# Differential attention in a four-layer fp32 stack: rotation side by side, one row maximum per head, four heads transposed by VectorE through DRAM

## The chip, the cores and the metric

The kernel runs on one core of a Trainium2 chip. The metric is the device time of one execution in microseconds. Three runs of the kernel before took 889.67, 889.81 and 889.84 us.

## The reference

The program is a stack of layers on 256 tokens of width 1024, all in fp32: gated linear attention, a feed-forward block, a gated projection, **differential attention**, a second feed-forward block and gated projection, a short convolution and a causal attention with ALiBi. The change lies in the differential attention, which is:

```python
q, k, v = split_cols(h @ w_in, [D_MODEL, D_MODEL, D_MODEL])
q = rms_norm(q.reshape(bsz, seq, nh, 2, dh), g_q)
k = rms_norm(k.reshape(bsz, seq, nh, 2, dh), g_k)
q = rope(...); k = rope(...)
lam = exp(sum(lam_q1 * lam_k1)) - exp(sum(lam_q2 * lam_k2)) + lambda_init
s = einsum('bhtqd,bhtkd->bhtqk', q_blk, kt) * scale
pr = softmax(s, axis=-1)
a = pr[:, :, 0] - lam * pr[:, :, 1]
o = einsum('bhqk,bhkd->bhqd', a, vt)
o = rms_norm(o, g_sub) * (1.0 - lambda_init)
return o.reshape(bsz, seq, D_MODEL) @ w_out
```

There are 8 heads (nh), each with two softmax maps of 256 x 256 (the index t, in the kernel m) over 64 columns, and values of 128 columns.

## The kernel before

**The weight stream.** Every matrix is cut into units of 256 rows by 512 columns (128 partitions x 1024 elements, 512 KB). For each unit SyncE loads `raw`, ScalarE rounds it to `whi` (L719, line function `split_to`), VectorE writes the rest `wlo = raw - whi` (L1130), and TensorE runs 12 matmuls of 512 columns (L1867, `product`): two row blocks and two column blocks of the activations, each as whi by hi, wlo by hi and whi by lo. ScalarE may not write a `whi` until TensorE is done with the unit 8 before it (RING = 8, semaphore `w_used`). A unit takes TensorE about 2.7 us, and there are 295.

**The order of the differential attention.** Its stage has 24 units of the input projection (six tiles of four: q, k, k, q, v, v halves) and 8 of the output projection. What else each engine has to do there is written out by hand in `DF_ORDER`: (u, step, argument) for each of TensorE (`pe`), ScalarE (`act`), VectorE (`dve`) and GpSimd (`pool`). TensorE does its steps ahead of unit u. ScalarE first writes `whi` up to unit u+6, VectorE `wlo` up to unit u+5, and then the step. Each engine runs its list strictly in that order, so a step that has to wait holds back all that stands behind it.

**The steps.** A tile of the projection (`tile`, L803 and L791) is squared and copied by ScalarE to `df_tok`. VectorE sums the squares (`sums`, L1524), GpSimd raises the sums to the power -0.5 (L644), and VectorE rotates the tile (`rope` and `more`: one row block of 128 tokens each, in `df_rope`, L1534 to L1554). For one row block this is two multiplications by the sine (256 elements, L1548), one by the cosine (512, L1552) and an addition (512, L1554), of which each kind waits for the one before it. k tiles are also scaled (`unit`, L1531). TensorE transposes the tiles (`qkT`, L2142), and ScalarE copies them from PSUM to `df_qkT` (L963).

Then, for each head: TensorE computes `scores` (L2156, eight matmuls into two banks, one per map); VectorE takes the maximum of each map (L1572, 512 elements from PSUM) and scales it (L1575); ScalarE runs four exponentials (L976, 256 elements each); VectorE combines the two maps (`soft`, L1582 to L1588); TensorE transposes the result (`aT`, L2167, four matmuls of 128 columns into bank 6); ScalarE copies it to `df_aT` (L984, `df_copy`), and TensorE multiplies by the values (`av`, L2182). Pairs of heads are then squared, copied and normalised (ScalarE's step `av`, `osums`, `norm`), transposed (`pair`, L1920) and split into hi and lo (ScalarE L730, VectorE L1146), and these are the left side of the output projection, whose first unit is u = 24.

**Banks.** Even heads use PSUM banks 4 and 5 for their scores, odd heads the pair of banks that the projection's other tiles leave free. Whoever writes a bank next waits for its reader (`claim`): the scores of head 2 for the exponentials of head 0, unit 24 for those of head 7, and so on.

**The other way to transpose.** The last attention of the stack already takes the probabilities of some of its heads (`MB_TRIPS`) another way: VectorE transposes blocks of 32 x 32 (L1740), GpSimd's queue writes the tile to DRAM (L673) and reads it back with the blocks in their new places (L681). `pair_blk` (L1171) does such a transpose of a 128 x 256 tile for the residual.

## Time and profile before

| | |
|---|---|
| median of three runs | 889.81 us (889.67 to 889.84) |
| profiled execution, span from first to last instruction | 888.3 us |
| median of the runs less that span | 1.5 us |
| busy: TensorE, VectorE, ScalarE, GpSimd | 99%, 76%, 57%, 8% |
| granted TensorE clock over the span | 1.000 |
| differential attention: first to last unit on TensorE | about 321 to 436 us |

A busy share is that of the time between an instruction's start and end in the trace. Instructions of one engine overlap a little: the next one's record starts before the last one's ends. So a cost is read from the start of one instruction to the start of the next. Times in the rows below are from the start of the span. "x4" in a timeline means that four instructions of one kind were merged into one row.

### The profile page before, as it was taken

What the parts mean: (1) busy time and instruction counts of PE and PEld (TensorE: products, weight loads), DVE (VectorE), ACT (ScalarE), POOL (GpSimd) and SP (SyncE); (2) the same over time, 40 slices, a digit from 0 to 9 for tenths busy, and PEclk for the clock granted to TensorE, in tenths of its full rate; (3) what the DMA queues carried; (4) which work ended last, traced back from release to release, by engine and by line L of the source; (5) the groups of instructions that cost most, each with busy time, mean ns of one, the idle gap of its engine ahead of it and who ended that gap; (6) DMA issues with size and microseconds to landing.
All of it is one profiled execution on the core that took longest, in us unless ns stands there. A gap on an engine that the chain in (4) does not pass through costs nothing.

```text
span 888.3 us, 12034 instructions
## 1 busy us (share of the span) xinstructions
PE 883.2 (99%) x4292; PEld 729.1 (82%) x4292; DVE 671.3 (76%) x1039; ACT 503.3 (57%) x822; POOL 75.4 (8%) x88
## 2 busy tenths in 40 slices
PE   9999999999999999999999999999999999999998
PEld 8988888888888878778888888888888888887777
DVE  6997688666746699997786666646879987789763
ACT  7656464444535576887564444444765444577581
POOL 1002000000000403111100000000010000115200
PEclk9999999999999999999999999999999999999999
DMA  9754578776666666433387667665787774857501
GB/s 341 263 179 176 203 260 297 251 267 246 241 213 237 213 227 246 144 103 112 131 300 265 250 235 255 244 233 178 254 296 261 239 245 144 300 175 238 186 26 48
DMA packets 85059, 193.72 MB, mean 218 GB/s; under 512 B 7236, under 2 KB 38340, under 8 KB 85000
## 3 DMA queue, kind: packets, MB, share of 16 engines
q1 hardware_dynamic: 83544, 189.15, 60.3%
q0 software_dynamic: 1024, 3.15, 1.0%
q8 instruction: 34, 0.56, 0.2%
q10 hardware_dynamic: 432, 0.66, 0.2%
q14 instruction: 25, 0.20, 0.1%
HBM read 174.84 MB, written 18.09 MB: 217 GB/s over the span
## 4 chain that ended last, share of the span: by engine, by line
PE 96%; DVE 1%; DMA 1%; ACT 0%; issue 0%; DVEq 0%; ACTq 0%
PE bank L1867 86%; PE bank L1905 3%; PE bank L2156 1%; PE bank L2182 1%; PE bank L2262 1%; PE bank L2292 1%; PE bank L1920 1%; DMA h<-x_dram 0%; DMA h_land<-residual_blocks 0%; PE bank L2167 0%; PE bank L2248 0%; PE bank L2067 0%; PE bank L2071 0%; PE bank L2142 0%; PE bank L2272 0%
## 5 line engine op out<-in xcount | busy, mean ns | idle before, releaser
L1130 DVE TENSOR_TENSOR wlo<-raw,whi 128x1024 fp32r<-128x1024 f32 x295 | 346.5, 1212 | 34.4 <-ACT whi L719 34.1
L719 ACT ACTIVATE whi<-raw 128x1024 fp32r<-128x1024 f32 x295 | 301.6, 1059 | 114.5 <-PE bank L1867 98.6
L1867 PE MATMUL bank<-whi,x_hi 128*128 128x512 f32 x560 | 152.4, 394 | 0.0
L1867 PE MATMUL bank<-wlo,x_hi 128*128 128x512 f32 x560 | 149.9, 389 | 0.0
L1867 PE MATMUL bank<-whi,x_lo 128*128 128x512 f32 x560 | 149.8, 389 | 0.0
L1867 PEld LDWEIGHTS bank<-wlo,x_hi 128*128 128x128 f32 x560 | 105.1, 188 | 22.2
L1867 PEld LDWEIGHTS bank<-whi,x_lo 128*128 128x128 f32 x560 | 105.1, 188 | 21.9
L1867 PEld LDWEIGHTS bank<-whi,x_hi 128*128 128x128 f32 x560 | 103.6, 188 | 22.5 <-issue 1.8
L1867 PE MATMUL bank<-whi,y_hi 128*128 128x512 f32 x396 | 107.6, 393 | 0.1
L1867 PE MATMUL bank<-whi,y_lo 128*128 128x512 f32 x396 | 106.1, 390 | 0.0
L1867 PE MATMUL bank<-wlo,y_hi 128*128 128x512 f32 x396 | 106.0, 389 | 0.0
L1867 PEld LDWEIGHTS bank<-whi,y_lo 128*128 128x128 f32 x396 | 74.3, 188 | 16.1 <-DVE y_lo L1146 0.5
L1867 PEld LDWEIGHTS bank<-wlo,y_hi 128*128 128x128 f32 x396 | 74.3, 188 | 15.7
L1867 PEld LDWEIGHTS bank<-whi,y_hi 128*128 128x128 f32 x396 | 73.1, 188 | 15.7 <-issue 0.8
L881 ACT ACTIVATE ffn_silu<-bank,rstd 128x256 f32<-128x256 f32 x44 | 18.4, 470 | 78.7 <-PE bank L1867 78.7
L1376 DVE SCALAR_TENSOR_TENSOR ffn_mid<-bank,rstd,ffn_silu 128x256 f32<-128x256 f32 x44 | 19.3, 479 | 54.9 <-ACT ffn_silu L881 54.7
L600 POOL TENSOR_TENSOR ms<-stats 128x2 f32<-128x2 f32 x8 | 4.9, 613 | 561.6 <-ACT junk L771 561.6
L1867 PE MATMUL bank<-whi,mid_hi 128*128 128x512 f32 x176 | 47.0, 389 | 0.0
L1867 PE MATMUL bank<-wlo,mid_hi 128*128 128x512 f32 x176 | 47.0, 389 | 0.0
L1867 PE MATMUL bank<-whi,mid_lo 128*128 128x512 f32 x176 | 47.0, 389 | 0.0
L1867 PEld LDWEIGHTS bank<-whi,mid_lo 128*128 128x128 f32 x176 | 33.0, 188 | 6.9
L1867 PEld LDWEIGHTS bank<-whi,mid_hi 128*128 128x128 f32 x176 | 33.0, 188 | 6.8
(260 smaller groups left out, 888.0 us busy)
## 6 DMA issues: line engine op xcount, KB each, us to landing
raw<-stream_dram SPq DMA_DIRECT2D x295, 512.0 KB, 4.6
ffn_blocks<-ffn_blk SPq DMA_DIRECT2D x22, 256.0 KB, 2.2
ffn_land<-ffn_blocks SPq DMA_DIRECT2D x22, 256.0 KB, 4.1
residual_blocks<-h_blk SPq DMA_DIRECT2D x20, 256.0 KB, 2.0
h_land<-residual_blocks SPq DMA_DIRECT2D x20, 256.0 KB, 2.8
cv_blocks<-cv_blk SPq DMA_DIRECT2D x7, 256.0 KB, 3.6
cv_land<-cv_blocks SPq DMA_DIRECT2D x7, 256.0 KB, 3.2
h_blocks<-h_blk SPq DMA_DIRECT2D x3, 512.0 KB, 2.9
```

The lines of the kernel that those rows point to most:

```text
L600: step(nc.gpsimd.tensor_tensor(ms[:, j, 0, :], stats[:, j, 0, :], stats[:, j, 1, :], ALU.add))
L719: A(whi[:, u % RING, :], raw[:, u % SLOTS, :], ACT.Copy).then_inc(sem("w_hi"), 1)
L881: A(sg[:, (t - tin) % 2, k, :], bank[2 * (t % 2) + k][:, 0:256], ACT.Silu, scale=rstd[:, j, k:k + 1]).then_inc(sem("ffn_silu"), 1)
L1130: V.tensor_tensor(wlo[:, u % SLOTS, :], raw[:, u % SLOTS, :], whi[:, u % RING, :].bitcast(F32), ALU.subtract).then_inc(sem("w_lo"), 1)
L1376: V.scalar_tensor_tensor(mid[:, (t - tin) % 2, :, k, :], bank[2 * (t % 2) + k][:, 256:512].rearrange("p (k n) -> p k n", k=2), rstd[:, j, ...
L1867: last = T.matmul(bank[pair + t][:, :], lhs[a][:, kt, t * P:(t + 1) * P], w[:, place(w, u), kk * NW:(kk + 1) * NW], start=part != 1 and k ...
L1905: last = T.matmul(bank[pair + hd // 2][:, hd % 2 * SEQ:(hd % 2 + 1) * SEQ], w[:, place(w, u), kk * NW + hd * P:kk * NW + (hd + 1) * P], lh ...
L1920: last = T.transpose(bank[b][:, k * SEQ + t * P:k * SEQ + (t + 1) * P], src[:, t, kt * P:(kt + 1) * P], ident)
L2156: last = T.matmul(bank[DF_S_BANKS[hd][m]][:, q * SEQ:(q + 1) * SEQ], dT[r, 0, hd, q * P:(q + 1) * P], dT[r, 1, hd, :], start=True, stop=True)
L2182: last = T.matmul(bank[b][:, q * SEQ + (hd % 2) * P:q * SEQ + (hd % 2 + 1) * P], daT[:, hd % 4, k * SEQ + q * P:k * SEQ + (q + 1) * P], dv ...
L2262: last = T.matmul(bank[MB_S_BANKS[i][m]][:, (0, P)[q]:(P, 3 * P)[q]], mT[r, 0, i, q * P:(q + 1) * P], mT[r, 1, i, 0:(q + 1) * P], start=Tr ...
L2292: last = T.matmul(bank[7][m * MB_HD:(m + 1) * MB_HD, c0 + k * P:c0 + SEQ], mv[:, k, hd * MB_HD:(hd + 1) * MB_HD], mpT[:, hd % 4, 2 * k * P ...
```

## The change

- **Trips.** The transposes of heads 0, 2, 3 and 4 on TensorE (16 of the 32) and their bank are dropped. VectorE transposes these heads' maps in blocks of 32 x 32 (`blk`, two instructions of 128 x 256 for each head), GpSimd's queue writes them to DRAM (`out`) and reads them back (`in`), 256 KB each way, and ScalarE copies them from the landing tile in SBUF to `df_aT` instead of from bank 6. The landing tile lies over a part of `x_lo`, and the tile that is written out over `p_hi` and `p_lo`.
- **Rotation.** `more` is gone: both row blocks of a tile are rotated in one step, the four sine multiplications first, then the two by the cosine, then the two additions. For tile 1 the step now stands behind `sums`, for tile 3 it stands whole ahead of head 1's `soft` and head 3's maximum.
- **Row maximum.** The eight banks become one PSUM tensor, and one reduction per head runs over both banks (1024 elements, four results), followed by one scaling. The exponentials of a head wait for both maps.
- **Order.** TensorE's `qkT` 5 moves next to `qkT` 4, and `aT` 1 from u = 18 to 19. ScalarE's copies of heads 0 to 4 move later: that of head 2 behind the exponentials of head 6, that of head 3 behind those of head 7, and that of head 4 behind `tile` 5 and `av` 3.
- The last attention's trips use the same semaphores and count on from the four new ones.

```diff
+DF_TRIPS = (0, 2, 3, 4)
+DF_TURNED = tuple(_h for _h in range(8) if _h not in DF_TRIPS)
...
 DF_ORDER = {
     "pe": (
         (1, "second", 0), (11, "qkT", 0), (11, "qkT", 1), (12, "qkT", 2), (13, "scores", 0), (13, "qkT", 3),
-        (13, "scores", 1), (16, "scores", 2), (16, "aT", 0), (18, "qkT", 4), (18, "scores", 3), (18, "aT", 1),
-        (19, "qkT", 5), (20, "qkT", 6), (20, "qkT", 7), (20, "scores", 4), (20, "aT", 2), (21, "scores", 5),
-        (21, "av", 0), (21, "aT", 3), (21, "av", 1), (21, "scores", 6), (22, "scores", 7), (22, "aT", 4),
+        (13, "scores", 1), (16, "scores", 2), (18, "qkT", 4), (18, "qkT", 5), (18, "scores", 3),
+        (19, "aT", 1), (20, "qkT", 6), (20, "qkT", 7), (20, "scores", 4), (21, "scores", 5),
+        (21, "av", 0), (21, "av", 1), (21, "scores", 6), (22, "scores", 7),
         (24, "pair", 0), (24, "av", 2), (24, "av", 3), (25, "aT", 5), (25, "av", 4), (25, "aT", 6), (25, "av", 5),
         (25, "aT", 7), (26, "pair", 1), (26, "av", 6), (26, "av", 7), (27, "pair", 2), (28, "pair", 3),),
     "act": (
         (5, "tile", 0), (8, "tile", 1), (11, "qkT", 0), (12, "qkT", 1), (12, "tile", 2), (12, "qkT", 2),
-        (13, "qkT", 3), (14, "scores", 0), (15, "scores", 1), (16, "tile", 3), (16, "aT", 0), (16, "scores", 2),
-        (18, "qkT", 4), (18, "aT", 1), (18, "scores", 3), (18, "qkT", 5), (19, "qkT", 6), (19, "qkT", 7),
-        (20, "tile", 4), (20, "scores", 4), (20, "aT", 2), (20, "scores", 5), (20, "aT", 3), (21, "av", 1),
-        (21, "scores", 6), (21, "aT", 4), (24, "scores", 7), (24, "pair", 0), (24, "tile", 5), (24, "av", 3),
-        (24, "aT", 5), (25, "aT", 6), (26, "av", 5), (26, "aT", 7), (26, "pair", 1), (27, "av", 7), (28, "pair", 2),
+        (13, "qkT", 3), (14, "scores", 0), (15, "scores", 1), (16, "tile", 3), (16, "scores", 2),
+        (18, "qkT", 4), (18, "qkT", 5), (18, "aT", 0), (18, "scores", 3), (19, "aT", 1), (19, "qkT", 6), (19, "qkT", 7),
+        (20, "tile", 4), (20, "scores", 4), (20, "scores", 5), (21, "av", 1),
+        (21, "scores", 6), (22, "aT", 2), (24, "scores", 7), (24, "aT", 3), (24, "pair", 0), (24, "tile", 5), (24, "av", 3),
+        (24, "aT", 4), (24, "aT", 5), (25, "aT", 6), (26, "av", 5), (26, "aT", 7), (26, "pair", 1), (27, "av", 7), (28, "pair", 2),
         (28, "pair", 3),),
     "dve": (
-        (5, "rope", 0), (6, "more", 0), (6, "sums", 0), (8, "rope", 1), (8, "sums", 1), (8, "more", 1),
-        (9, "unit", 1), (11, "sums", 2), (11, "rope", 2), (11, "more", 2), (11, "scores", 0), (12, "scores", 1),
-        (13, "soft", 0), (16, "unit", 2), (17, "scores", 2), (17, "soft", 1), (17, "rope", 3), (17, "scores", 3),
-        (17, "sums", 3), (17, "more", 3), (18, "soft", 2), (19, "scores", 4), (19, "soft", 3), (19, "scores", 5),
-        (19, "soft", 4), (21, "scores", 6), (22, "osums", 0), (22, "scores", 7), (22, "norm", 0), (22, "soft", 5),
+        (5, "rope", 0), (6, "sums", 0), (8, "sums", 1), (8, "rope", 1),
+        (9, "unit", 1), (11, "sums", 2), (11, "rope", 2), (11, "scores", 0), (12, "scores", 1),
+        (13, "soft", 0), (13, "blk", 0), (16, "unit", 2), (17, "scores", 2), (17, "rope", 3), (17, "soft", 1), (17, "scores", 3),
+        (17, "sums", 3), (18, "soft", 2), (18, "blk", 2), (19, "scores", 4), (19, "soft", 3), (19, "blk", 3), (19, "scores", 5),
+        (19, "soft", 4), (19, "blk", 4), (21, "scores", 6), (22, "osums", 0), (22, "scores", 7), (22, "norm", 0), (22, "soft", 5),
         (22, "soft", 6), (23, "pair", 0), (23, "osums", 1), (23, "soft", 7), (24, "norm", 1), (25, "osums", 2),
         (25, "pair", 1), (26, "norm", 2), (27, "osums", 3), (27, "norm", 3), (27, "pair", 2), (28, "pair", 3),),
     "pool": (
-        (4, "sums", 0), (8, "sums", 1), (12, "sums", 2), (16, "sums", 3), (21, "osums", 0), (24, "osums", 1),
+        (4, "sums", 0), (8, "sums", 1), (12, "sums", 2), (13, "out", 0), (14, "in", 0), (16, "sums", 3), (18, "out", 2), (19, "out", 3), (19, "in", 2),
+        (20, "in", 3), (20, "out", 4), (21, "osums", 0), (21, "in", 4), (24, "osums", 1),
         (26, "osums", 2), (28, "osums", 3),),
 }
+DF_COPIED = tuple(arg for _, step, arg in DF_ORDER["act"] if step == "aT")
...
-        bank = [ctx.enter_context(nc.psum_tensor(f"bank{b}", [P, NW], F32)) for b in range(8)]
+        psum = ctx.enter_context(nc.psum_tensor("bank", [P, 8, NW], F32))
+        bank = [psum[:, b, :] for b in range(8)]
...
+        sb("under_df_land", [P, 3 * D], scope=landing)
+        aland = sb("df_land", [P, 2, NW], scope=landing)
...
+        ablk = sb("df_blk", [P, 2, NW], scope=staging)
...
+            def df_out(hd):
+                n = DF_TRIPS.index(hd)
+                pool.wait_ge(sem("mb_blk"), n + 1)
+                nc.gpsimd.dma_start(a_dram[n], ablk[:, n % 2, :]).then_inc(sem(f"mb_out{n % 2}"), 16)
+            def df_in(hd):
+                n = DF_TRIPS.index(hd)
+                pool.wait_ge(sem(f"mb_out{n % 2}"), 16 * (n // 2 + 1))
+                if n >= 2:
+                    pool.wait_ge(sem("df_aT"), DF_COPIED.index(DF_TRIPS[n - 2]) + 1)
+                nc.gpsimd.dma_start(aland[:, n % 2, :].rearrange("p (i w) -> p i w", i=P // B),
+                                    a_dram[n].rearrange("q n -> (q n)").rearrange("(i p w) -> p i w", i=P // B, p=P))\
+                    .then_inc(sem(f"mb_land{n % 2}"), 16)
...
+            def turned_aside(hd):
+                if hd in DF_TRIPS:
+                    act.wait_ge(sem("mb_blk"), DF_TRIPS.index(hd) + 1)
+                else:
+                    act.wait_ge(sem("df_aT_filled"), DF_TURNED.index(hd) + 1)
             def df_exp(hd):
                 if DF_P_AFTER[hd] is not None:
-                    act.wait_ge(sem("df_aT_filled"), DF_P_AFTER[hd] + 1)
+                    turned_aside(DF_P_AFTER[hd])
                 elif hd == 6:
                     act.wait_ge(sem("df_rope"), TT * 4)
                 for m in range(2):
-                    act.wait_ge(sem("df_max"), 4 * hd + 2 * (m + 1))
+                    act.wait_ge(sem("df_max"), 2 * (hd + 1))
...
             def df_copy(hd):
-                act.wait_ge(sem("df_aT_filled"), hd + 1)
                 if hd >= 4:
                     act.wait_ge(sem("df_av"), hd - 3)
+                if hd in DF_TRIPS:
+                    n = DF_TRIPS.index(hd)
+                    act.wait_ge(sem(f"mb_land{n % 2}"), 16 * (n // 2 + 1))
+                    A(daT[:, hd % 4, :].rearrange("p (n i b) -> p n i b", n=4, b=B),
+                      aland[:, n % 2, :].rearrange("p (i n b) -> p n i b", n=4, b=B), ACT.Copy).then_inc(sem("df_aT"), 1)
+                    return
+                act.wait_ge(sem("df_aT_filled"), DF_TURNED.index(hd) + 1)
                 A(daT[:, hd % 4, :], bank[6][:, :], ACT.Copy).then_inc(sem("df_aT"), 1)
...
-            def df_rope(t, k):
+            def df_rope(t):
                 w = (0, 1, 1, 0)[t]
-                for k in (k,):
-                    xt = dtok[:, t % 2, k, :]
-                    x5 = xt.rearrange("p (a m u e) -> p a m u e", a=4, m=2, u=2)
+                for k in range(TT):
+                    x5 = dtok[:, t % 2, k, :].rearrange("p (a m u e) -> p a m u e", a=4, m=2, u=2)
                     m5 = dm2[:, k, :].rearrange("p (a m u e) -> p a m u e", a=4, m=2, u=2)
                     sn = rot[:, w, 1, k, :].rearrange("p (m u e) -> p m u e", m=2, u=2)
-                    cs = rot[:, w, 0, k, :].unsqueeze(1).to_broadcast([P, 4, P])
-                    x3 = xt.rearrange("p (a e) -> p a e", a=4)
                     dve.wait_ge(sem("df_in"), TT * t + k + 1)
                     if t:
                         dve.wait_ge(sem("df_rope"), TT * (t - 1) + k + 1)
@@ -1548,8 +1591,13 @@
                         V.tensor_tensor(m5[:, :, :, u, :], x5[:, :, :, 1 - u, :],
                                         sn[:, :, u, :].unsqueeze(1).to_broadcast([P, 4, 2, HD2]), ALU.mult)\
                             .then_inc(sem("df_swap"), 1)
+                for k in range(TT):
+                    x3 = dtok[:, t % 2, k, :].rearrange("p (a e) -> p a e", a=4)
                     dve.wait_ge(sem("df_swap"), 2 * (TT * t + k + 1))
-                    V.tensor_tensor(x3, x3, cs, ALU.mult).then_inc(sem("df_cos"), 1)
+                    V.tensor_tensor(x3, x3, rot[:, w, 0, k, :].unsqueeze(1).to_broadcast([P, 4, P]), ALU.mult)\
+                        .then_inc(sem("df_cos"), 1)
+                for k in range(TT):
+                    xt = dtok[:, t % 2, k, :]
                     dve.wait_ge(sem("df_cos"), TT * t + k + 1)
                     V.tensor_tensor(xt, xt, dm2[:, k, :], ALU.add).then_inc(sem("df_rope"), 1)
@@ -1564,16 +1612,18 @@
             def df_max(hd):
                 stt = dstat[:, hd, :]
-                factors = dqr[:, hd // 4, :].rearrange("p (q a m) -> p q a m", q=TT, a=4)
+                factors = dqr[:, hd // 4, :].rearrange("p (q a m) -> p a m q", q=TT, a=4)
                 if hd % 4 == 0:
                     dve.wait_ge(sem("df_rstd"), TT * (1, 4)[hd // 4])
-                for m in range(2):
-                    dve.wait_ge(sem("df_scores"), 2 * hd + m + 1)
-                    V.tensor_reduce(stt[:, 2 * m:2 * m + 2], bank[DF_S_BANKS[hd][m]][:, :].rearrange("p (q k) -> p q k", q=TT),
-                                    AXX, ALU.max).then_inc(sem("df_max"), 1)
-                    dve.wait_ge(sem("df_max"), 4 * hd + 2 * m + 1)
-                    V.scalar_tensor_tensor(stt[:, 4 + 2 * m:6 + 2 * m], stt[:, 2 * m:2 * m + 2], -1.0,
-                                           factors[:, :, hd % 4, m], ALU.mult, ALU.mult).then_inc(sem("df_max"), 1)
+                b = DF_S_BANKS[hd][0]
+                dve.wait_ge(sem("df_scores"), 2 * (hd + 1))
+                V.tensor_reduce(stt[:, 0:4].rearrange("p (m q) -> p m q", m=2),
+                                psum[:, b:b + 2, :].rearrange("p m (q k) -> p m q k", q=TT), AXX, ALU.max)\
+                    .then_inc(sem("df_max"), 1)
+                dve.wait_ge(sem("df_max"), 2 * hd + 1)
+                V.scalar_tensor_tensor(stt[:, 4:8].rearrange("p (m q) -> p m q", m=2),
+                                       stt[:, 0:4].rearrange("p (m q) -> p m q", m=2), -1.0,
+                                       factors[:, hd % 4, :, :], ALU.mult, ALU.mult).then_inc(sem("df_max"), 1)
...
+            def df_blocks(hd):
+                n = DF_TRIPS.index(hd)
+                dve.wait_ge(sem("df_a"), TT * (hd + 1))
+                if n >= 2:
+                    dve.wait_ge(sem(f"mb_out{n % 2}"), 16 * (n // 2))
+                for q in range(TT):
+                    last = V.transpose(ablk[:, n % 2, :].rearrange("p (f k q b) -> p q f k b", f=P // B, q=TT, b=B)[:, q],
+                                       DF_P[hd][:, 0, q, :].rearrange("p (k b f) -> p f k b", b=B, f=P // B))
+                last.then_inc(sem("mb_blk"), 1)
```

## Rows read from the trace of the kernel before

**Rows 1.** The page: the chain that ended last, shares of the span by engine.
```profile
PE 96%; DVE 1%; DMA 1%; ACT 0%; issue 0%; DVEq 0%; ACTq 0%
```

**Rows 2.** Timeline of TensorE: start us, us, engine, line, operation, count, idle before.
```profile
386.10 1.14 PE L2156 MATMUL bank<-df_qkT 64*128 64x256 f32 x8 [0.25 <-ACT df_qkT L963]
...
398.03 1.13 PE L2156 MATMUL bank<-df_qkT 64*128 64x256 f32 x8
399.10 0.66 PE L2167 MATMUL bank<-consts,df_p 128*128 128x128 f32 x4
399.51 1.17 PE L1867 MATMUL bank<-whi,y_hi 128*128 128x512 f32 x4
...
405.50 1.95 PE L2182 MATMUL bank<-df_v,df_aT 128*128 128x128 f32 x16
407.21 1.17 PE L1867 MATMUL bank<-whi,x_hi 128*128 128x512 f32 x4
```

**Rows 3.** Timeline of ScalarE, same columns as rows 2.
```profile
356.70 1.27 ACT L791 ACTIVATE df_tok<-bank,rstd 128x512 f32<-128x512 f32 x2
...
377.81 2.00 ACT L719 ACTIVATE whi<-raw 128x1024 fp32r<-128x1024 f32 x2
...
380.65 0.59 ACT L976 ACTIVATE df_o<-bank,df_stat,df_q_rstd 128x256 f32<-128x256 f32 x1
...
385.44 1.09 ACT L963 ACTIVATE df_qkT<-bank 128x512 f32<-128x512 f32 x2 [1.04 <-PE bank L2142]
...
397.79 0.56 ACT L976 ACTIVATE df_m<-bank,df_stat,df_q_rstd 128x256 f32<-128x256 f32 x1 [0.33 <-DVE df_stat L1575]
...
400.45 3.22 ACT L719 ACTIVATE whi<-raw 128x1024 fp32r<-128x1024 f32 x3
403.57 0.55 ACT L976 ACTIVATE df_p<-bank,df_stat,df_q_rstd 128x256 f32<-128x256 f32 x1
...
405.74 0.84 ACT L730 ACTIVATE x_hi<-bank,cols 128x256 fp32r<-128x256 f32 x2
```

**Rows 4.** Timeline of VectorE, same columns.
```profile
357.63 0.75 DVE L1548 TENSOR_TENSOR df_m<-df_tok,df_rot 128x256 f32<-128x256 f32 x2
358.41 0.69 DVE L1552 TENSOR_TENSOR df_tok<-df_tok,df_rot 128x512 f32<-128x512 f32 x1
359.13 0.69 DVE L1554 TENSOR_TENSOR df_tok<-df_tok,df_m 128x512 f32<-128x512 f32 x1
359.74 0.75 DVE L1548 TENSOR_TENSOR df_m<-df_tok,df_rot 128x256 f32<-128x256 f32 x2
...
361.86 0.68 DVE L1572 TENSOR_REDUCE df_stat<-bank 128x2 f32<-128x512 f32 x1
...
363.45 1.22 DVE L1130 TENSOR_TENSOR wlo<-raw,whi 128x1024 fp32r<-128x1024 f32 x1
...
381.28 1.30 DVE L1524 TENSOR_REDUCE df_ss<-df_sq 128x8 f32<-128x520 f32 x2
...
391.68 0.69 DVE L1572 TENSOR_REDUCE df_stat<-bank 128x2 f32<-128x512 f32 x1 [0.60 <-PE bank L2156]
...
398.41 1.22 DVE L1130 TENSOR_TENSOR wlo<-raw,whi 128x1024 fp32r<-128x1024 f32 x1
...
431.60 1.14 DVE L1171 STREAM_TRANSPOSE h_blk<-h 128x256 f32<-128x256 f32 x2
```

**Rows 5.** Stretch: us, busy PE, PEld, DVE, ACT, POOL (instructions), clock, DMA share, GB/s.
```profile
357.60:399.80 42.20, 41.95 (x234) 32.27 (x233) 40.41 (x83) 35.56 (x86) 6.41 (x4) 1.00 0.35 121
```

**Rows 6.** Groups by line with shapes kept apart: count, busy us, mean ns, idle before.
```profile
L741 ACT ACTIVATE y_hi<-h_land,cols 128x256 fp32r<-128x256 f32 x12 | 5.5, 503 | 9.0 <-DMA h_land<-residual_blocks 9.0
...
L1727 DVE TENSOR_REDUCE mb_stat<-mb_s 128x1 f32<-128x128 f32 x16 | 4.6, 286 | 0.6
```

**Rows 7.** DMA issues by line: KB each, median us from issue to landing.
```profile
mb_blocks<-p_tok POOLq DMA_DIRECT2D x8, 192.0 KB, 3.4
mb_pT<-mb_blocks POOLq DMA_DIRECT2D x8, 192.0 KB, 4.1
```

More of the change, by code:

```diff
@@ L651, in df_onorm @@
                     .then_inc(sem("df_orstd"), 1)
-            for _, what, arg in df_order("pool"):
-                if what == "sums":
+            def df_out(hd):
[10 more added lines that the diff above has]
+                    .then_inc(sem(f"mb_land{n % 2}"), 16)
+            for _, what, arg in df_order("pool"):
+                if what == "out":
+                    df_out(arg)
+                elif what == "in":
+                    df_in(arg)
+                elif what == "sums":
                     for k in range(TT):
@@ L1611, in _ @@
                     head_sums(arg, dsq65, dss, "df_sq", "df_ss", "df_rstd")
-                elif step in ("rope", "more"):
-                    df_rope(arg, step == "more")
+                elif step == "rope":
+                    df_rope(arg)
                 elif step == "unit" and arg in (1, 2):
@@ L1622, in _ @@
                     df_soft(arg)
+                elif step == "blk":
+                    df_blocks(arg)
                 elif step == "osums":
@@ L1734, in mb_blocks @@
             def mb_blocks(hd):
-                n = MB_TRIPS.index(hd)
+                n = len(DF_TRIPS) + MB_TRIPS.index(hd)
                 dve.wait_ge(sem("mb_exp"), TT * (hd + 1))
@@ L2280, in mb_av @@
                 if 2 * i in MB_TRIPS:
-                    pair = MB_TRIPS.index(2 * i) // 2
+                    pair = (len(DF_TRIPS) + MB_TRIPS.index(2 * i)) // 2
                     pe.wait_ge(sem(f"mb_land{pair % 2}"), 2 * 16 * (pair // 2 + 1))
```

21 lines of the change are left out of this document (13 added, 8 removed).

## The prediction

> **What bounds the kernel now.** I read the page's chain first: TensorE carries 96% of it [rows 1], so one microsecond taken off TensorE in the attention stage is one gained, and one for which TensorE must wait is one lost. Then I read TensorE's own timeline in the stage. It stands still once, ahead of head 4's scores, for ScalarE's copy of transpose 6: the copy starts at 385.44 and the scores at 386.10 [rows 2, 3]. Nothing else there waits. Last I read the engines that feed it. From the rotation of tile 2 at 357.63 to the last maximum before 398.41, VectorE has one pause, 0.60 us ahead of head 5's maximum, and is busy 40.41 of 42.20 us [rows 4, 5]. So VectorE paces the chain of small steps, although TensorE does not notice yet. The tight place is unit 24, the first of the output projection. Its weights start at 407.21 [rows 2]; it needs head 7's exponentials out of the banks, which end at 405.74, and the first pair's hi parts, which ScalarE writes from 405.74 on [rows 3]: 0.84 us, so until 406.6. The slack is 0.6 us.
>
> **The change, part by part.**
>
> *TensorE.* After a head's scores a transpose takes 399.10 to 399.51, 0.41 us [rows 2]. Four go: -1.66 us (a fourth one, between two products with the values, costs much the same). Moving transpose 5 next to 4 I put at nothing; it saves or costs one change of operation, 0.1 us.
>
> *Rotation.* An instruction that reads the one before it starts 0.03 us after that one's end (357.63 + 0.75 = 358.38, start 358.41; 358.41 + 0.69 = 359.10, start 359.13); one that does not starts 0.08 us ahead of the end (359.13 + 0.69 = 359.82, start 359.74) [rows 4]. Side by side, all four dependences of a tile are covered: -4 x 0.11 = -0.44 us for each tile. The Trainium skill ("VectorE: DVE Perf Modes", section "The DRAIN you can't avoid") says that the next instruction does not start until the pipe is empty, and that chaining without semaphores gains nothing; by that the rotation would save nothing. The trace does not bear it out here, since the addition's successor started ahead of its end; I keep -0.44.
>
> *Maximum.* A head's two now take 361.86 to 363.45, 1.59 us [rows 4]. A reduction takes 0.286 us for 128 elements [rows 6] and 0.68 for 512, 1.03 ns an element, so an estimated 1.21 for 1024; with the dependent scaling 1.21 + 0.03 + 0.08 = 1.32. That is -0.27 a head. Bounds: no saving in the reduction beyond one scaling and its edges (-0.2), or half of the fixed part again (-0.35). But the first exponential now waits for both maps.
>
> *Blocks.* Two transposes of 128 x 256 take 1.14 us [rows 4]; behind the softmax they are dependent: 1.14 - 0.08 + 0.11 = 1.17 a head, four times.
>
> *Copies.* From PSUM, 512 elements follow each other in 0.49 us (two in 1.09) [rows 3]. From a landing tile in SBUF only 256 are seen, 0.503 us [rows 6]. To the 1024 of a whi copy (two in 2.00, so 1.05 each, 0.95 apart) [rows 3] it rises by 0.71 ns an element: 0.69 us, 0.59 to the next. Bounds 0.49 and 0.95; I take 0.59, the row with the same broken pattern.
>
> *Trips.* 3.4 us out and 4.1 back for 192 KB [rows 7]; here 256 KB, so an estimated 3.4 to 4.5 and 4.1 to 5.5. GpSimd's list is in order: `in` 2 waits behind `out` 3, which goes when head 3's blocks are done, at 392.4 by the sum below; it lands by 398. Head 3's own waits for its `out`: 402.4 at the latest. ScalarE comes for the two at 403.0 and 407.7 (below). Head 4's has some 1.5 us to spare (rival 4). GpSimd's powers for tile 3 come 10 us after `in` 0 and lose nothing. I take nothing for trips. SyncE's queue is unchanged; the four last-attention trips that share semaphores wait for counts long reached.
>
> *Start of the count.* The sums of tile 1 now wait for GpSimd's powers of tile 0, which eats what rotations 0 and 1 save. Rotation 2 cannot start before ScalarE writes the tile, 356.70 to 357.97 [rows 3], so I start at 357.63 as before, -0.2 to +0.5.
>
> *VectorE up to head 6's maximum.* It ended at 398.41 [rows 4]. Rotations 2 and 3: -0.88. Seven maxima: -1.89. Blocks of heads 0, 2, 3, 4: +4.68. The pause of 0.60 [rows 4] goes. Together +1.31: 399.72. Splits for units 25 and 26 still stand ahead of it. The exponentials of head 6 follow about 0.18 later, at 399.9, against 397.79 [rows 3]. That is the step which pays: ScalarE has nothing else it may do, since its next whi stands behind them.
>
> *ScalarE from there to unit 24.* Four exponentials 2.17 (403.57 to 405.74) [rows 3]: 402.07. One whi 0.95: 403.02. Copy of head 2, 0.59: 403.61. Two whi 1.90: 405.51 (before, three took 3.12 because the last waited for unit 22; by now that is long done). Head 7's exponentials 2.17: 407.68. Copy of head 3, new in this place, 0.69: 408.37. TensorE can then do `av` 3, eight of the sixteen matmuls that took 405.50 to 407.21 [rows 2], 0.86 us, 0.05 after the copy: unit 24 at 409.28. The pair's hi parts come at 408.27 + 0.84 = 409.11 and do not decide.
>
> So unit 24 starts **2.07 us later** than 407.21, though TensorE had 1.66 us less to do. A second stall lies on the way: rotation 3 ahead of head 3's maximum, which ended at 381.28 [rows 4]. Its second half +2.12 (357.63 to 359.74 is one half [rows 4]), blocks of head 0 +1.17, rotations -0.88, four maxima -1.08: 382.61. Exponentials 382.8 instead of 380.65 [rows 3], +2.17, whi +0.95, copy of head 1 +0.49, copy of transpose 6 +0.66: head 4's scores at 387.1 instead of 386.10. With the transposes gone this alone would put unit 24 at 407.21 + 0.94 - 1.24 = 406.9. It is inside the 2.07, not beside it: the later of the two chains decides. Behind unit 24 the spacing stays, and TensorE has no slack in which to make it up.
>
> The sum: 889.81 + 2.07 = **891.9 us**. The durations are of one execution with a span of 888.3 us; the runs lie 1.5 us above it, and I add the difference to their median. For this forecast alone I put 890.9 to 893.0 (reductions +-0.08 for each of seven heads, copies between their bounds, start of the count).
>
> **The rivals.**
>
> 1. *TensorE alone decides.* VectorE and ScalarE keep up and neither wait appears: -1.66 us, 888.2. This is the gain side. For it: VectorE's list has grown by only 1.3 us in 42. Against: head 6's exponentials would have to start by 399.9 - 2.07 - 1.66 = 396.2, ahead of where they start today, with 4.68 us more to do. To come past 0.2% the wait at head 4's scores would have to shrink too. 0.16, of which 0.09 beyond 0.2%.
>
> 2. *Only the first stall.* Copies or blocks come cheaper, so that `av` 3 does not wait, but head 4's scores still do: 406.9 for unit 24, -0.3, 889.5. It needs head 6's exponentials by 397.5. Everything from here to the forecast is a mixture of the two. 0.22.
>
> 3. *Dependences cost the same wherever they stand.* In rows: the second cosine and the additions start 0.03 us after the end of the one ahead, not 0.08 before it; rotations 2 and 3 save nothing, +0.88 in front of head 6, 892.8. The rows above speak against it. The Trainium skill's page "VectorE: DVE Perf Modes" states it in the section "The DRAIN you can't avoid". 0.08.
>
> 4. *A trip lands late.* Head 4's `in` waits for ScalarE's copy of head 2 (done 403.7) and lands 4.1 to 5.5 later, 409.2 with GpSimd's issue to add. ScalarE wants it behind the pair (0.8), tile 5 (1.2, as 356.70 shows) and two passes over a bank (1.0) after 408.3 [rows 3]: 411.3. If it slips by 3 us, the copy of head 4 and `av` 4 behind it come some 1.5 later: 893.4. 0.06.
>
> The forecast itself has 0.48.
>
> **How the numbers follow.** A measurement of this kernel can tell about 0.2%, 1.78 us, from no change: slower means above 891.6, faster below 888.0. The forecast's 0.48 lies above 891.6 in some two thirds (0.31), 3 and 4 wholly (0.14), and of the mixture next to nothing: slower 0.45. Rival 1 gives faster 0.09. The rest, 0.46, is within 0.2%. The range leaves out the outer half of rival 1 and the slip beyond 893.2: 888.6 to 893.2.
>
> **What would show it.** Right: a wait of TensorE on `df_aT` ahead of `av` 3, of 2 us or more, and one of about 1 us more than before on `df_qkT`; head 6's exponentials at about 399.9 after an idle ScalarE that waits for `df_stat`; VectorE without a pause from 357 to 400; tiles in SBUF before ScalarE reaches their copies; one reduction at 1.2 us. Wrong: no wait at `av` 3; head 6's exponentials before 398; a DMA named as what ended ScalarE's wait; reductions of two banks that cost clearly other than 1.2 us, or a rotation that takes 4.2 us as before.

## The result and the profile after

The changed kernel took **893.22 us** in the median (891.34 to 893.83, 6 runs) against 889.83 us (889.65 to 890.24, 6 runs) of the kernel before beside it: ratio 1.0030, 95% interval [1.0020, 1.0039]. That is 3.4 us slower, at the upper edge of the range given (893.2). The runs fall in two bunches, 891.34 and 891.61 us at a mean granted clock of 1.000, and 893.1 to 893.5 at 0.998; the profiled one (893.83 us, span 892.0) belongs to neither, for a reason of its own below.

In the page's chain TensorE's share fell from 96% [rows 1] to 90%, and VectorE's rose from 1% to 7%:

```profile
PE 90%; DVE 7%; issue 1%; ACT 1%; DMA 1%; POOL 0%; ACTq 0%; DVEq 0%
```

The timeline of TensorE in the attention stage, changed kernel (start us, us, engine, line, operation, count, idle before and who ended it); the first row is unit 11's weights, the last unit 24's:

```profile
354.50 1.17 PE L1930 MATMUL bank<-whi,y_hi 128*128 128x512 f32 x4
...
383.68 0.63 PE L2230 MATMUL bank<-consts,df_p 128*128 128x128 f32 x4 [0.28 <-ACT df_qkT L996]
...
388.60 0.63 PE L2205 MATMUL bank<-consts,df_tok 128*128 128x128 f32 x4 [1.08 <-ACT df_aT L1030]
389.15 1.13 PE L2219 MATMUL bank<-df_qkT 64*128 64x256 f32 x8
...
407.29 1.06 PE L2245 MATMUL bank<-df_v,df_aT 128*128 128x128 f32 x8
410.34 1.16 PE L2245 MATMUL bank<-df_v,df_aT 128*128 128x128 f32 x8 [1.99 <-ACT df_aT L1026]
411.27 1.16 PE L1930 MATMUL bank<-whi,x_hi 128*128 128x512 f32 x4
```

Where before there was one pause of 0.25 us [rows 2] there are three: 0.28 us ahead of head 1's transposes, 1.08 us ahead of transpose 7 (its bank is held by head 1's transposed map until ScalarE has copied it), and 1.99 us ahead of head 3's product with the values, for the copy of head 3. From unit 11's weights to unit 24's it takes 411.27 - 354.50 = **56.77 us**. Before, unit 11's weights started at 352.48 and unit 24's at 407.21 [rows 2]: 54.73. I call this the stretch from here on; it is what a run changed in the stage, whatever came before. Unit 11 in the kernel before:

```profile
352.48 1.17 PE L1867 MATMUL bank<-whi,y_hi 128*128 128x512 f32 x4
```

What made the copy late is read backwards on ScalarE (same columns):

```profile
401.93 0.57 ACT L1016 ACTIVATE df_m<-bank,df_stat,df_q_rstd 128x256 f32<-128x256 f32 x1 [1.72 <-DVE df_stat L1624]
...
405.06 0.63 ACT L1026 ACTIVATE df_aT<-df_land 128x512 f32<-128x512 f32 x1
405.57 2.01 ACT L752 ACTIVATE whi<-raw 128x1024 fp32r<-128x1024 f32 x2
407.47 0.56 ACT L1016 ACTIVATE df_p<-bank,df_stat,df_q_rstd 128x256 f32<-128x256 f32 x1
...
409.63 0.65 ACT L1026 ACTIVATE df_aT<-df_land 128x512 f32<-128x512 f32 x1
```

Head 6's exponentials (401.93) waited 1.72 us for VectorE's maximum; everything down to the copy of head 3 at 409.63 then runs without a pause. On VectorE:

```profile
359.68 1.42 DVE L1591 TENSOR_TENSOR df_m<-df_tok,df_rot 128x256 f32<-128x256 f32 x4
361.01 1.28 DVE L1597 TENSOR_TENSOR df_tok<-df_tok,df_rot 128x512 f32<-128x512 f32 x2
362.22 1.28 DVE L1602 TENSOR_TENSOR df_tok<-df_tok,df_m 128x512 f32<-128x512 f32 x2
363.42 1.21 DVE L1620 TENSOR_REDUCE df_stat<-bank 128x4 f32<-128x1024 f32 x1
364.67 0.17 DVE L1624 SCALAR_TENSOR_TENSOR df_stat<-df_stat,df_q_rstd 128x4 f32<-128x4 f32 x1
364.75 1.22 DVE L1176 TENSOR_TENSOR wlo<-raw,whi 128x1024 fp32r<-128x1024 f32 x1
...
397.09 1.16 DVE L1648 STREAM_TRANSPOSE df_blk<-df_p 128x256 f32<-128x256 f32 x2
398.18 2.32 DVE L1176 TENSOR_TENSOR wlo<-raw,whi 128x1024 fp32r<-128x1024 f32 x2
400.41 1.22 DVE L1620 TENSOR_REDUCE df_stat<-bank 128x4 f32<-128x1024 f32 x1
```

The three kinds of step can be priced here against [rows 4]: a rotation takes 363.42 - 359.68 = 3.74 us, a head's maximum 364.75 - 363.42 = 1.33 us. Head 6's maximum starts at 400.41, behind head 4's blocks and two splits.

**The start of this execution.** Unit 11 came 2.02 us later than before (354.50 against 352.48), though nothing that TensorE runs before it was changed. It comes from the first microseconds. Changed kernel:

```profile
1.17 3.78 PE L2029 MATMUL bank<-gla_r 128*128 128x256 f32 x8 [1.17 <-DVE gla_r L1261]
5.82 1.09 PE L1983 MATMUL bank<-consts,h 128*128 128x128 f32 x4 [0.86 <-DMA h<-x_dram]
6.70 1.92 PE L2039 MATMUL bank<-gla_r 128*128 128x256 f32 x4
8.05 2.27 PE L1968 MATMUL bank<-x_hi,whi 128*128 128x256 f32 x8
```

Kernel before:

```profile
5.28 1.01 PE L1920 MATMUL bank<-consts,h 128*128 128x128 f32 x4 [0.32 <-DMA h<-x_dram]
6.13 1.03 PE L1976 MATMUL bank<-gla_r 128*128 128x256 f32 x4
6.94 1.22 PE L1905 MATMUL bank<-x_hi,whi 128*128 128x256 f32 x8
```

The first tile landed 0.54 us later, the same four products then took 1.92 us instead of 1.03, and the eight behind them 2.27 instead of 1.22. A second profile of the same changed kernel (E12) starts like the kernel before, so I take 2.02 us off the times of this profile when I compare them with the prediction's.

### The profile page after: what moved, and what is told of

It reads as the page before. It is cut to its first block, busy times and chain, and to the rows that moved or that the text cites. A ratio compares the mean times of both kernels' runs of the same rounds, so it can differ in the third digit from the quotient of the medians.

```text
span 892.0 us, 12004 instructions
## 1 busy us (share of the span) xinstructions
PE 883.8 (99%) x4276; PEld 729.0 (82%) x4276; DVE 672.8 (75%) x1031; ACT 504.1 (57%) x822; POOL 81.8 (9%) x96
## 4 chain that ended last, share of the span: by engine, by line
PE 90%; DVE 7%; issue 1%; ACT 1%; DMA 1%; POOL 0%; ACTq 0%; DVEq 0%
PE bank L1930 81%; PE bank L1968 3%; DVE wlo L1176 2%; DVE df_stat L1620 1%; PE bank L2325 1%; PE bank L2355 1%; DVE df_m L1591 1%; PE bank L1983 1%; DMA h<-x_dram 1%; DVE df_tok L1597 1%; PE bank L2245 1%; POOL df_q_rstd L657 0%; DVE df_blk L1648 0%; DVE df_tok L1602 0%; PE bank L2311 0%
```

## The experiments

All times are medians, and each ratio is against runs of the kernel before on the same chip. Four chips were used: one for E1 to E4, one for E5 to E8, one for E9 and E10, one for E11 and E12; the medians of the kernel before on them are 890.10, 889.97, 889.74 and 889.79 us. "Stretch" is read from each run's own trace.

**E1. More warm-up products.** Do the late start of the profile and the two bunches of runs have one cause?

```
-WARM, KEEP = 4, 2
+WARM, KEEP = 6, 2
```

> The changed kernel with six warm-up products instead of four ahead of the first load; nothing else. In the trace of the changed kernel TensorE waited 0.86 us for the first tile instead of 0.32, and the products after it took twice as long: the attention stage (weights of unit 11) began at 354.50 instead of 352.48 us. Theory: the gap before the first tile is what costs, and two thirds of the excess is slow products. Filled, unit 11 begins within 0.7 us of 352.48 and all runs lie within 0.6 us of 891.6. Rival: the late landing of the first tile itself costs 2 us whatever TensorE does before it: median stays at 893.2 with some runs at 891.4.

Measured: unit 11 at 352.34 us, as the theory had it (E12, without the edit, begins there too, so this does not show that the two products did it), but the stretch unchanged (56.78, with the wait of 1.98) and the runs still in bunches: 891.37 to 892.60 at clock 1.000 (7 runs), 893.59 to 894.30 at 0.998 (4 runs), median 892.38, ratio 1.0027 [1.0018, 1.0036]. The second half of the theory is refuted: the bunches don't come from the start.

**E2. No trips.** `DF_TRIPS = ()`, TensorE's and ScalarE's lists of the kernel before, VectorE's of the changed one without `blk`.

> The changed kernel with no head turned by VectorE: all eight are transposed by TensorE, with TensorE's and ScalarE's order of the kernel before; rotation side by side and one maximum per head stay. From the start of unit 11's weights to that of unit 24's it was 54.73 us before and 56.77 in the changed kernel. Theory (the blocks on VectorE make the chain late): the stretch comes back to 54.4 to 54.8, no wait ahead of the products with the values, head 6's exponentials some 3 us nearer to unit 11 than in the changed kernel, and the time is 889.3 to 889.9 if the start is as before, up to 2 us more if the late start is not a matter of the trips. Rival (rotation or the joint maximum is what delays): the stretch stays above 56 us.

Measured: 891.94 us, ratio 1.0022 [1.0013, 1.0032], stretch 56.64. By number the rival's value, but the trace names another cause:

```profile
380.45 0.66 PE L2229 MATMUL bank<-consts,df_p 128*128 128x128 f32 x4 [1.79 <-DVE df_p L1637]
```

TensorE waited 1.79 us for head 1's softmax, which the changed list puts behind the whole rotation of tile 3, while TensorE's list of before asks for it ahead of unit 18 instead of unit 19. The wait ahead of the products with the values was gone. The experiment mixed two orders that don't fit; E7 mends it. It also shows what head 1's transposes would have waited for had the change left them where they were.

**E3. Only the first wait taken away.** ScalarE copies head 1 ahead of head 3's exponentials.

```
-... (18, "aT", 0), (18, "scores", 3), (19, "aT", 1), ...
+... (18, "aT", 0), (18, "aT", 1), (18, "scores", 3), ...
```

> The changed kernel with one step moved on ScalarE: the copy of head 1's transposed map stands ahead of head 3's exponentials. TensorE waited 1.08 us for that copy ahead of transpose 7, and 1.99 us ahead of head 3's product with the values. Theory (the later of two chains decides, and VectorE sets the second): the first wait falls below 0.3, the second grows by as much as the first lost, to about 3 us; the stretch from unit 11 to unit 24 stays within 0.3 of 56.77 us, and so does the time, within 0.04% of the changed kernel for the same start. Rival (the two waits add up): the stretch loses 1.1 us, 55.7, and the time with it.

Measured: stretch 56.69 (expected within 0.3 of 56.77), 892.42 us, ratio 1.0026 [1.0016, 1.0036], four runs at clock 1.000 at 891.37 to 891.77 us, like those of the changed kernel, three at 0.998 at 893.08 to 893.71, and one at 1.000 and 893.17, which no profile explains.

```profile
386.52 1.13 PE L2219 MATMUL bank<-df_qkT 64*128 64x256 f32 x8 [0.66 <-ACT df_qkT L996]
...
408.17 1.16 PE L2245 MATMUL bank<-df_v,df_aT 128*128 128x128 f32 x8 [2.44 <-ACT df_aT L1026]
```

The first wait shrank from 1.08 to 0.66 (it went to the scores, since the copy of transpose 6 stands behind the same exponentials; I had expected under 0.3), and the second grew by 0.45. Their sum stays, 3.07 and 3.10. **The waits don't add up**: the later chain decides, and what TensorE wins ahead of it is waited away at its end.

**E4. Only the second chain shortened.** On VectorE head 6's maximum goes ahead of head 4's blocks and two splits.

```
-... (19, "soft", 4), (19, "blk", 4), (21, "scores", 6), ...
+... (19, "soft", 4), (19, "scores", 6), (19, "blk", 4), ...
```

> The changed kernel with one step moved on VectorE: head 6's maximum stands ahead of head 4's blocks and two splits instead of behind them. Theory (VectorE's order makes head 6's exponentials late, and they the copy of head 3): they follow ScalarE's own work at once, 1.7 us sooner; the wait ahead of head 3's product with the values falls from 1.99 to about 0.3, the stretch from unit 11 to unit 24 from 56.77 to 55.1 us, and the time by 1.7 us, to about 891.5 with the late start and 889.7 without it. Rival (ScalarE's own load or the landing of a trip sets the copy): no change of the wait and the time, 893.2.

Measured: **889.83 us** (889.59 to 890.52, 11 runs, none below clock 1.000), ratio 0.9998 [0.9990, 1.0007]; stretch 54.93.

```profile
352.25 1.17 PE L1930 MATMUL bank<-whi,y_hi 128*128 128x512 f32 x4
...
406.25 1.16 PE L2245 MATMUL bank<-df_v,df_aT 128*128 128x128 f32 x8 [0.15 <-ACT df_aT L1026]
407.18 1.16 PE L1930 MATMUL bank<-whi,x_hi 128*128 128x512 f32 x4
```

The wait fell from 1.99 to 0.15, as expected within 0.2 us. One line of VectorE's order is worth the whole loss, and more than the 1.84 us of the stretch: the runs at 0.998 are gone too.

**E5. All three waits attacked by order alone**, same work as the changed kernel: ScalarE takes copies and head 7's exponentials ahead of splits of weights, VectorE takes the maxima of heads 4, 6 and 7 ahead of blocks and splits.

> The changed kernel, same work, with steps of ScalarE and VectorE reordered so that none of TensorE's three waits of the stage should be left. ScalarE: copies of transposes 4 and 5 straight behind head 2's exponentials, copy of head 1 ahead of head 3's exponentials, copies of transposes 6 and 7 straight behind them, copy of head 3, head 7's exponentials and the hi parts of the first pair ahead of two splits of weights. VectorE: head 4's maximum ahead of one split, head 6's ahead of head 4's blocks, head 7's ahead of two splits. Theory (TensorE's four transposes less are worth their 1.66 us where nothing is late): the stretch from unit 11 to unit 24 falls to 53.2 to 53.6 us (54.73 before), no wait of over 0.3 us in it, and the time is 888.1 to 888.6, 1.2 to 1.7 us below the kernel before. Rival (VectorE is too full for the whole chain whatever the order): a new wait of 0.5 us or more, stretch above 54.2.

Measured: 889.93 us, ratio 0.9997 [0.9988, 1.0006], stretch 54.29: a miss on both, and by number the rival's value; E9 shows that VectorE is not too full. New waits took the place of the old ones. On the way to unit 24:

```profile
404.32 0.66 PE L1983 MATMUL bank<-consts,df_o 128*128 128x128 f32 x4 [0.70 <-DVE df_o L1664]
```

The pair's norm now stood behind head 7's maximum and two splits. And unit 25 followed unit 24 after 6.91 us instead of 6.03. In the trace some 0.3 us of that lie ahead of unit 24's third group, for the pair's lo parts, which VectorE wrote behind a split, and some 0.4 ahead of head 5's transposes, for a copy that ScalarE did behind two splits and tile 5.

**E6. A longer wait**, for the bunches: ScalarE copies head 3 behind the pair's hi parts and tile 5.

```
-... (24, "aT", 3), (24, "pair", 0), (24, "tile", 5), ...
+... (24, "pair", 0), (24, "tile", 5), (24, "aT", 3), ...
```

> The changed kernel with ScalarE's copy of head 3 behind the hi parts of the first pair and tile 5: the wait ahead of head 3's product with the values grows from 1.99 to about 3.9 us. It asks why runs of the changed kernel fall in two bunches: 891.3 to 891.7 where the mean granted clock is 1.000, 893.1 to 893.5 where it is 0.998. Theory (TensorE's idle stretch of 2 us is followed by a lower clock in about half of the executions, and in none where the wait was 0.15 us): with the longer wait nearly all executions show 0.998 or less, at 895 to 896 us; where the profile holds one, the products after the wait take about twice as long for some 3 to 4 us at a granted clock below 1. Rival (the start of the program makes the bunches): the share of runs at 0.998 stays as it was, and the rest lie at 893.4.

Measured: 895.92 us, ratio 1.0064 [1.0051, 1.0076], all 5 runs at a clock of 0.998 or 0.996. The wait was 3.87 us. The profile by stretches (us; busy us and count of TensorE, weight loads, VectorE, ScalarE, GpSimd; granted clock; DMA share; GB/s):

```profile
406.00:408.00 2.00, 0.11 (x2) 0.00 (x0) 0.93 (x1) 2.00 (x8) 0.00 (x0) 1.00 0.84 326
408.00:410.00 2.00, 0.01 (x1) 0.01 (x1) 0.88 (x2) 1.93 (x4) 0.00 (x0) 0.79 0.07 27
410.00:412.00 2.00, 2.00 (x9) 2.00 (x10) 0.00 (x0) 0.00 (x0) 0.00 (x0) 0.50 0.00 0
...
414.00:416.00 2.00, 2.00 (x6) 1.61 (x5) 2.00 (x4) 0.00 (x0) 0.64 (x1) 0.50 0.00 0
416.00:420.00 4.00, 4.00 (x32) 3.61 (x32) 1.65 (x2) 2.77 (x4) 0.00 (x0) 1.00 0.39 133
```

TensorE is idle from 406, its granted clock falls to 0.50, the level of 1.2 GHz, and comes back to 1.00 by 416, after some 6 us of work. (The share of executions fits the theory; that the low clock would last 3 to 4 us was too short.)

**E7. No trips, with head 1's transposes and transpose 5 where the changed kernel has them.**

> All eight heads transposed by TensorE, as in the run before without trips, but with head 1's transposes and transpose 5 where the changed kernel has them, so that head 1's softmax, which stands behind the whole rotation of tile 3, has time: its wait of 1.79 us should go. Theory (the blocks on VectorE make head 6 late; the wait ahead of transpose 7 comes from the order alone): no wait ahead of the products with the values, the wait ahead of transpose 7 stays near 1.1 us, the stretch from unit 11 to unit 24 is 55.3 to 55.8, the time 890.4 to 891.0, and no run at a clock of 0.998. Rival (rotation or the joint maximum makes head 6 late as well): a wait of 1 us or more ahead of the products with the values stays.

Measured: 890.68 us (889.73 to 892.09, 11 runs, all at clock 1.000), ratio 1.0009 [1.0000, 1.0018], stretch 54.79, no wait at all in it. The time lies in the expected range by luck, since the stretch is 0.5 us below its own: five of the runs are at 891.4 to 892.1 us at clock 1.000, which no profile explains, and the other six at 889.73 to 890.68. So rotation and joint maximum delay nothing, and neither do they win anything for TensorE. That the wait ahead of transpose 7 would stay was wrong: without head 0's blocks, and with its transposes back on TensorE, head 3's exponentials start 381.79 - 379.02 = 2.77 us after unit 18's weights instead of 384.73 - 380.39 = 4.34, and the copy of head 1 is in time. That wait came with the trips too.

**E8. The order of E5 without trips.**

> The reordered steps of the first kernel of this call, but all eight heads transposed by TensorE. It prices the trips where nothing is late. Theory (four transposes of 0.41 us each): the stretch is 54.6 to 55.2 and the time 889.4 to 890.0, some 1.3 to 1.7 us above the reordered kernel with trips. Rival (the order alone makes the gain, the trips nothing): the two are within 0.3 us.

Measured: 891.29 us (890.69 to 892.72, 11 runs), ratio 1.0016 [1.0007, 1.0025], stretch 55.20. The time misses the expectation by 1.3 us; in its profile the start is late again (unit 11 at 353.92), and the order has E5's fault (unit 25 is 6.91 us behind unit 24, 0.88 more than before). What the start adds in its other runs no profile shows. Against E5 on the same chip it is 1.36 us slower, with a stretch 0.91 longer; E11 prices the trips without these faults.

**E9. The order mended where E5's trace showed new waits**: on VectorE head 5's maximum goes ahead of head 3's blocks, the pair's sums and norm ahead of two splits and its lo parts ahead of one; on ScalarE one split less stands ahead of tile 5, and head 3's copy stands behind head 7's exponentials again.

> The reordered kernel with trips, mended where its own trace showed new waits: the row sums and the norm of the first pair stood behind two splits on VectorE (0.70 us ahead of the pair's transposes), and tile 5 with the copy after it stood behind two splits on ScalarE, which took the 0.44 us won at unit 24 back by unit 25. Now VectorE does head 5's maximum ahead of head 3's blocks, the pair's sums, head 7's maximum and the pair's norm ahead of two splits, the pair's lo parts ahead of one; ScalarE does one split between the copy of head 3 and the pair's hi parts and one behind the copy of head 4. Theory (TensorE's four transposes less are worth 1.66 us where nothing is late): the stretch from unit 11 to unit 24 falls to 53.2 to 53.8 us, unit 25 follows 6.0 to 6.2 us later, and the time is 888.1 to 888.9. Rival (what is taken from one wait appears in another, since VectorE has no pause): the stretch is 54 or more, or unit 25 comes over 6.5 us later, and the time stays at 889.5 or above.

Measured: **888.35 us** (888.18 to 890.31, 11 runs, all at clock 1.000), ratio **0.9985 [0.9977, 0.9994]**, faster than both kernels; stretch 53.29, unit 25 6.18 us behind unit 24, and one wait left in the stage, the 0.25 us that was there before.

```profile
352.49 1.18 PE L1930 MATMUL bank<-whi,y_hi 128*128 128x512 f32 x4
...
403.64 0.60 PE L1983 MATMUL bank<-consts,df_o 128*128 128x128 f32 x4
404.07 1.95 PE L2245 MATMUL bank<-df_v,df_aT 128*128 128x128 f32 x16
405.78 1.17 PE L1930 MATMUL bank<-whi,x_hi 128*128 128x512 f32 x4
...
411.96 1.18 PE L1930 MATMUL bank<-whi,x_hi 128*128 128x512 f32 x4
```

The sixteen products of heads 2 and 3 run through again, as in [rows 2].

**E10. As E9, with tile 5 and two copies behind the second split on ScalarE.**

> As the one before, but tile 5, the copy after it and the copy of head 4 stand behind the second split of weights on ScalarE, as they did in the first reordered kernel. Theory: the split's 0.95 us delays the copy of head 4 by as much; unit 24 comes as in the kernel before, unit 25 up to 0.8 us later, and the time is up to 0.8 us longer. Rival (the copies there have slack): the two are within 0.2 us.

Measured: 888.29 us, ratio 0.9988 [0.9979, 0.9997], stretch 53.32: within 0.1 us of E9. The rival is right, there is slack in that place once the pair's sums, norm and lo parts come early. So the two splits alone did not cost E5 its 0.88 us; which of its placements did was not told apart.

**E11. The order of E9 without trips.**

> The mended order of the kernel that ran at 888.35 us, but all eight heads transposed by TensorE and no blocks on VectorE (the copies of heads 0, 2, 3 and 4 come from PSUM again). Theory (the trips are worth what TensorE no longer does, about 0.41 us a head, and the order alone nothing): the stretch from unit 11 to unit 24 is 54.6 to 55.0 us and the time 889.4 to 890.0, 1.2 to 1.6 above the one with trips. Rival (the order makes the gain): within 0.4 us of 888.35.

Measured: 889.77 us (889.39 to 890.15), ratio 1.0000 [0.9992, 1.0009], stretch 54.80.

```profile
352.74 1.17 PE L1929 MATMUL bank<-whi,y_hi 128*128 128x512 f32 x4
...
407.54 1.17 PE L1929 MATMUL bank<-whi,x_hi 128*128 128x512 f32 x4
```

**Order, rotation and joint maximum together win nothing, the trips are worth about 1.4 us**: 889.77 - 888.35 = 1.42, on two chips; 1.37 when each is taken against the kernel before on its own chip; 1.51 in the stretch. But they are worth it only in an order in which their 4.9 us on VectorE make nothing late.

**E12. The changed kernel again.**

> The changed kernel once more, unaltered. Its profile began 2 us late at the first load, and its runs fell in two bunches. Theory (the late start belongs to that execution, the bunches to the clock after the wait of 2 us ahead of head 3's product with the values): in the profile unit 11 begins at 352.2 to 352.8 us, the stretch to unit 24 is 56.8 us with the same wait, and runs at a mean granted clock of 1.000 lie at 891.3 to 892.6, those at 0.998 at 893.0 to 894.3, about a third to a half of all. Rival (the changed program starts late as a rule): unit 11 begins after 354 again.

Measured: 893.12 us (891.40 to 893.66, 6 runs), ratio 1.0033 [1.0020, 1.0045]; unit 11 at 352.26, stretch 56.79. Three runs at 0.998 (893.05, 893.19, 893.66), two at 891.40 and 891.74, and one at clock 1.000 and 893.41, which no profile explains. This time the profiled execution is one at 0.998. TensorE's timeline, and the stretches:

```profile
352.26 1.17 PE L1930 MATMUL bank<-whi,y_hi 128*128 128x512 f32 x4
...
408.09 1.19 PE L2245 MATMUL bank<-df_v,df_aT 128*128 128x128 f32 x8 [1.98 <-ACT df_aT L1026]
409.05 2.02 PE L1930 MATMUL bank<-whi,x_hi 128*128 128x512 f32 x4
410.86 1.84 PE L1930 MATMUL bank<-wlo,x_hi 128*128 128x512 f32 x4
412.55 1.08 PE L1930 MATMUL bank<-whi,x_lo 128*128 128x512 f32 x4
...
416.75 1.18 PE L1930 MATMUL bank<-whi,x_hi 128*128 128x512 f32 x4
```

```profile
406.00:408.00 2.00, 0.11 (x1) 0.00 (x0) 0.92 (x1) 2.00 (x8) 0.00 (x0) 1.00 0.89 340
408.00:409.00 1.00, 0.91 (x8) 0.92 (x8) 0.20 (x1) 1.00 (x4) 0.00 (x0) 1.00 0.04 16
409.00:410.00 1.00, 1.00 (x5) 0.82 (x4) 0.67 (x2) 1.00 (x3) 0.00 (x0) 0.54 0.00 0
410.00:411.00 1.00, 1.00 (x4) 0.79 (x3) 0.47 (x1) 1.00 (x4) 0.00 (x0) 0.50 0.00 0
...
412.00:413.00 1.00, 1.00 (x4) 0.75 (x4) 1.00 (x3) 0.00 (x0) 0.35 (x1) 0.76 0.00 0
```

After the same wait of 1.98 us the clock falls to 0.50 within the first microsecond of unit 24, and the first two groups take 2.02 and 1.84 us instead of 1.16 and about 1.08 (from start to start 1.81 and 1.69 us, where the kernel before has 1.00 and 0.92). Unit 25 comes 416.75 - 409.05 = 7.70 us behind unit 24, where the first profile of the same program has 6.13: **1.57 us**, about the distance between the bunches.

## Why the prediction was right in its mechanism and short in its size

With 2.02 us taken off the first profile, step by step:

| step of the prediction | predicted | measured |
|---|---|---|
| rotation of a tile | -0.44 us | 3.74 against 4.23: -0.49 |
| maximum of a head | -0.27, one reduction 1.21 | 1.33 against 1.59: -0.26, reduction 1.21 to 1.24 |
| head 4's scores | 387.1 | 389.15 - 2.02 = 387.13 |
| end of head 6's maximum (the next start) | 399.72 | 401.74 - 2.02 = 399.72 |
| head 6's exponentials | 399.9 | 401.93 - 2.02 = 399.91 |
| a copy from SBUF, to the next start | 0.59 | 405.57 - 405.06 = 0.51 |
| copy of head 3, start | 407.68 | 409.63 - 2.02 = 407.61 |
| unit 24 | +2.07 | 56.77 - 54.73 = +2.04 |

*What bounds it.* That VectorE paces the chain and that unit 24 is where it shows was right; E4 shows it by moving one maximum. That the second, not the first, of the two late chains decides ("inside the 2.07, not beside it") is E3's result. That the end of head 6's maximum agrees to 0.01 us is luck on that scale: the blocks came to 1.20 to 1.24 us a head instead of 1.17, 0.18 more in all, and the two rotations saved 0.10 more than predicted, the maxima 0.07 less.

*The first stall* came at the right time and of the right size, but by another way than written: not the copy of transpose 6 but the copy of head 1 held it, and the longer wait on `df_qkT` that was to show it is one on `df_aT`. Both kernels put head 1's transposes and transposes 5 and 7 into bank 6. Before, transpose 5 stood between; now transpose 7 comes straight behind head 1's transposes in that bank and needs their copy. Head 3's late exponentials stand ahead of both copies.

*Trips* at nothing was right: the copies of heads 2 and 3 did not wait for a landing. They landed in 3.4 to 3.8 us on the way back, below the 4.1 to 5.5 that I had bounded from the smaller trips of [rows 7]; rival 4 did not occur.

*Rival 3* (dependences cost the same anywhere): refuted by the 3.74 us of a rotation. The prediction took from the Trainium skill's "VectorE: DVE Perf Modes", section "The DRAIN you can't avoid", only that the next instruction waits for the pipe to empty, by which the rotation would have kept its 4.23. The same paragraph goes on: "A next op that is not held starts earlier". The traces agree with that sentence: in [rows 4] an instruction that does not read the one before it starts 0.08 us ahead of that one's end.

*Rivals 1 and 2* (TensorE alone decides; only the first stall) did not occur in this order. E9 is rival 1 brought about by another order: where nothing is late, the stretch is 1.44 us shorter than before, against the 1.66 put down for the four transposes.

**The step that failed** is the last but one: "Behind unit 24 the spacing stays". At full clock it nearly stayed (unit 25 6.13 us behind unit 24 in the first profile, 6.03 before), and there the kernel takes 891.34 to 891.74 us, a little under the 891.9 forecast (the later wait of 0.41 us on VectorE's `mb_s` that the kernel before has is gone in the changed one). In half of the executions of the changed kernel (6 of 12) the clock was lower, and in the one of them that has a profile the spacing grew by 1.57 us more, because TensorE went on at half its clock after the wait. I had priced the wait at its own length and nothing more. 2.04 + 0.10 + 1.57 - 0.41 = 3.30 us is about what the upper bunch shows (893.1 to 893.7 in both sets of runs, against 889.8), and with half of the runs at the low clock, and one each lifted there by something else (the late start; the run at 893.41), the median falls into it. The likeliest case's own range ended at 893.0, so it missed by 0.2 us. That the median lies at the edge of the whole range, and not inside it at about 891.5, is for this reason partly a matter of chance: with the same wait, E1's median is 892.38.

How often it happened, counted by a mean granted clock below 1.000, by the longest wait of TensorE inside the stage: none of 92 executions of the kernel before (0.25 us), none of 77 of E4, E5 and E7 to E11 (up to 1.08 us), 1 of 9 at 1.79 us (E2), 10 of 23 at 1.98 or 1.99 us (changed kernel, E1, E12), 3 of 8 at 2.44 us (E3), 5 of 5 at 3.87 us (E6). E4 (0 of 11) ran on the chip of E1 to E3, and E5, E7 and E8 (0 of 33) on that of E6, so it is not the chip.

**The late start** of the first profile is a second, separate thing of nearly the same size. Of the profiled executions it hit that one and E8's, and E12 shows the same program without it. That runs of the kernel before at 891.2 to 892.0 us and clock 1.000 (7 of the 92) are the same thing is likely, but no profile holds one.

## What to carry to other kernels

Work taken off the bounding engine and laid on one that "has time" is worth what the bounding engine gives up only if the receiving engine's order is rearranged with it: here the change cost 3.4 us as placed, and ran 1.4 us faster than the kernel before in an order that kept maxima ahead of blocks and splits. When a trace shows several waits on one engine, shorten the chain that ends last first (E4, one line) and expect the others to surface: E3, which shortened another, won nothing, and E5, which went at all three, ran no faster than E4. And a wait of the matmul engine like the one of 2 us here should be priced with a second term for the clock behind it.
